# Three more seven-product groups and a shorter drain of the low banks in a hybrid decoder layer on one core

## The reference

```
hdn    = square(relu(x1 @ w_ff1))          # 256 x 8192, w_ff1 2048 x 8192
ff_out = hdn @ w_ff2                       # 256 x 2048, w_ff2 8192 x 2048
out    = layer_norm(ALPHA * x1 + ff_out)
```

## Time and profile before

| | |
|---|---|
| median of three runs | 1090.41 us (1090.23 to 1090.50) |
| the profiled execution, its time | 1090.53 us |
| the profiled execution, its span | 1088.5 us |
| PE busy | 1083.7 us of the span |
| DVE busy | 809.6 us, 74% |
| ACT busy | 571.7 us, 53% |
| mean HBM rate | 196 GB/s |

### The profile page before, as it was taken

How to read it: one execution, slowest core, us unless ns; L and a number is a source line. 1 busy time by engine, 2 the same in 40 slices (tenths; PEclk the granted TensorE clock), 3 DMA queues, 4 the chain that set the end, 5 groups by cost and what they waited for, 6 DMA issues and landing times.

```text
span 1088.5 us, 13897 instructions
## 1 busy us (share of the span) xinstructions
PE 1083.7 (100%) x5595; PEld 920.1 (85%) x5595; DVE 809.6 (74%) x890; ACT 571.7 (53%) x723; POOL 24.6 (2%) x43
## 2 busy tenths in 40 slices
PE   9999999999999999999999999999999999999998
PEld 8888888888888888888888888888888888888886
DVE  6587757666656685676699898666776678889998
ACT  6487757565554524445465454344454455554561
POOL 1000101010000000000000000000000000000000
PEclk9999999999999999999999999999999999999999
DMA  9857655557555825665756557466656655655762
GB/s 304 262 181 223 188 182 160 177 177 240 174 163 169 291 93 167 188 188 177 228 176 231 194 195 243 155 190 189 190 176 208 209 181 195 231 193 192 279 224 78
DMA packets 108047, 213.83 MB, mean 196 GB/s; under 512 B 6784, under 2 KB 38016, under 8 KB 107472
## 3 DMA queue, kind: packets, MB, share of 16 engines
q1 hardware_dynamic: 107216, 209.61, 59.5%
q0 software_dynamic: 624, 3.21, 1.0%
q10 hardware_dynamic: 144, 0.13, 0.0%
HBM read 210.83 MB, written 2.10 MB: 196 GB/s over the span
## 4 chain that ended last, share of the span: by engine, by line
PE 98%; DVE 1%; DMA 0%; issue 0%; ACT 0%; DVEq 0%
PE low_ps L797 11%; PE low_ps L634 10%; PE high_ps L797 9%; PE high_ps L817 8%; PE high_ps L818 8%; PE high_ps L819 8%; PE low_ps L526 6%; PE low_ps L522 6%; PE low_ps L524 6%; PE low_ps L803 5%; PE high_ps L803 5%; PE low_ps L639 5%; PE low_ps L817 2%; PE low_ps L818 2%; PE low_ps L819 2%; PE high_ps L571 1%
## 5 line engine op out<-in xcount | busy, mean ns | idle before, releaser
L1303 DVE TENSOR_TENSOR w_lo<-w_raw,w_hi 128x1024 fp32r<-128x1024 f32 x175 | 213.3, 1223 | 134.9 <-ACT w_hi L976 133.4
L976 ACT ACTIVATE w_hi<-w_raw 128x1024 fp32r<-128x1024 f32 x175 | 185.2, 1059 | 189.5 <-PE low_ps L526 68.9
L797 PE MATMUL low_ps<-x1T,w_hi 128*128 128x512 f32 x512 | 177.3, 393 | 0.0
L797 PE MATMUL high_ps<-x1T,w_hi 128*128 128x512 f32 x448 | 155.0, 393 | 0.0
L634 PE MATMUL low_ps<-xT,w_hi 128*128 128x512 f32 x448 | 144.2, 398 | 0.0
L803 PE MATMUL low_ps<-x1T,w_lo 128*128 128x256 f32 x512 | 139.3, 278 | 0.0
L1627 DVE TENSOR_TENSOR w_lo<-w_raw,w_hi 128x1024 fp32r<-128x1024 f32 x72 | 87.1, 1223 | 64.6 <-ACT w_hi L1175 64.6
L1175 ACT ACTIVATE w_hi<-w_raw 128x1024 fp32r<-128x1024 f32 x72 | 76.1, 1059 | 88.8 <-PE low_ps L797 43.4
L803 PE MATMUL high_ps<-x1T,w_lo 128*128 128x256 f32 x448 | 122.1, 278 | 0.0
L818 PE MATMUL high_ps<-w_lo,hid 128*128 128x512 f32 x290 | 112.4, 388 | 0.0
L819 PE MATMUL high_ps<-w_hi,hid 128*128 128x512 f32 x290 | 112.4, 388 | 0.0
(11 more groups left out here) (218 smaller groups left out, 1908.0 us busy)
## 6 DMA issues: line engine op xcount, KB each, us to landing
w_raw<-in_w_ff SPq DMA_DIRECT2D x208, 512.0 KB, 4.4
w_raw<-in_w_in SPq DMA_DIRECT2D x93, 512.0 KB, 4.1
more_raw<-in_w_ff SPq DMA_DIRECT2D x42, 512.0 KB, 5.3
w_raw<-in_w_out SPq DMA_DIRECT2D x32, 512.0 KB, 3.7
x_raw<-in_x_turned SPq DMA_DIRECT2D x8, 256.0 KB, 6.3
y<-in_x SPq DMA_DIRECT2D x8, 256.0 KB, 4.5
side_raw<-in_w_ff SPq DMA_DIRECT2D x4, 512.0 KB, 7.0
w_raw<-in_w_in SPq DMA_DIRECT2D x6, 256.0 KB, 5.2
```

Source lines behind the costliest of these rows:

```text
L797: return pe.matmul(banks[:, b, :], w_hi[:, slot, cols], x1T[:, t, :, :].rearrange("p h t -> p (h t)"), start=(t == 0 and not lows_open), s ...
L976: act.activation(w_hi[:, slot, :], w_raw[:, slot, :], ACT.Copy).then_inc(w_rounded, units)
L1303: dve.tensor_tensor(w_lo[:, slot, :], w_raw[:, slot, :], w_hi[:, slot, :].bitcast(F32), ALU.subtract).then_inc(w_split, units)
```

## The change

Thirty pairs are fast instead of 27: chunk 1 gives both of its pairs (`DOUBLE`), and the exception for the chunk `MIXED` falls, so passes 0 to 3 have 7, 7, 8 and 8 fast pairs. Since plain pairs fill the places between, a pass now ends in one plain pair where pass 0 ended in three: pass 0 runs F4 p0 F6 p2 F10 p8 F14 p12 F18 p16 F22 p20 F26 p24, and pass 1 opens with F4. Pass 2 ends F58 p62, where it ended F54 p58 p60 p62, and pass 3, which opens with F30, is as before.

The drain is in two steps. `copy_first` waits for the second mark of the last fast pair, after its fifth product, not the third. `drain_low` is three operations into a larger `mid` and frees the banks; `add_low`, one operation of 128 x 2048, adds `mid` to `y1` later (in passes 1 and 3 five or six pairs into the pass, for the one before). The scaling by `ALPHA` moves into `add_high`. In `end_pass` the splits of the last plain pair come ahead of the drain, and the splits of the next plain pair are put among the high additions. `small`, `ident_t`, `diag` and some buffers move in memory.

```diff
-MIXED = CHUNKS_FF - 2
-BLOCKS = [12 if c == MIXED else 11 if c in FAST_CHUNKS else 8 for c in range(CHUNKS_FF)]
+DOUBLE = 1
+FAST_PAIRS = [t for c in FAST_CHUNKS for t in ((TPC * c, TPC * c + 2) if c == DOUBLE else (TPC * c + 2,))]
+BLOCKS = [2 * TPC + 3 * len([t for t in FAST_PAIRS if t // TPC == c]) for c in range(CHUNKS_FF)]
...
         def copy_first(p):
 
-            act.wait_ge(fast_used, 3 * FAST_END[p])
+            act.wait_ge(fast_used, 3 * FAST_END[p] - 1)
             if p:
-                act.wait_ge(low_drained, p)
-            act.activation(mid[:, 0, :], low_ps[:, 0, :], ACT.Copy).then_inc(first_copied, 1)
+                act.wait_ge(low_added, p)
+            act.activation(mid[:, 1, :], low_ps[:, 0, :], ACT.Copy).then_inc(first_copied, 1)
+
+        def next_pass(p):
+
+            q = PASS_END[p]
+            round_pair(q - 1)
+            copy_first(p)
+            round_sums(q)
+            round_own(q)
...
         def drain_low(p):
 
+            dve.wait_ge(first_copied, p + 1)
+            dve.tensor_tensor(mid[:, 0, :], mid[:, 1, :], low_ps[:, 3, :], ALU.subtract).then_inc(
+                mid_made, 1)
+            dve.wait_ge(mid_made, 2 * p + 1)
+            dve.tensor_tensor(mid[:, 3, :], mid[:, 0, :], low_ps[:, 2, :], ALU.subtract).then_inc(
+                mid_made, 1)
+            dve.wait_ge(mid_made, 2 * p + 2)
+            dve.tensor_tensor(mid[:, 0:4:2, :], low_ps[:, 1:2, :].to_broadcast([P, 2, NC]),
+                              mid[:, 0:4:3, :], ALU.subtract).then_inc(low_drained, 1)
...
+        def add_low(p):
+
+            dve.wait_ge(low_drained, p + 1)
+            if p < len(PASSES) - 1:
+                dve.wait_ge(y2_summed, 3 * (p + 1))
+            mine = y1[:, :, half_of(p)]
+            dve.tensor_tensor(mine, mine, mid[:, :, :].rearrange("p (t b) n -> p t (b n)", t=TT),
+                              ALU.add).then_inc(low_added, 1)
...
+        HIGH = [(3, 1), (0, 2), (2, 1)]
 
         def end_pass(p):
 
             q = PASS_END[p]
+            split_pair(q - 1)
             drain_low(p)
             sum_pair(q)
-            split_pair(q - 1)
             split_sums(q)
             split_own(q)
-            add_high(p)
+            add_high(p, HIGH[:2])
+            split_plain(q + 1, (0,))
+            add_high(p, HIGH[2:])
+            split_plain(q + 1, (1,))
...
         for q in range(6, PART_END):
+            if q == PASS_START[1] + 6:
+                add_low(0)
             if q == PASS_END[0] - 1:
                 end_pass(0)
-            elif q == PASS_END[1] - 1:
-                drain_low(1)
+            elif q not in (PASS_START[1], PASS_START[1] + 1):
                 split_pair(q)
-            elif q != PASS_START[1]:
-                split_pair(q)
+        drain_low(1)
```

More of the change, by code:

```diff
@@ L80, in pass_order @@
     tiles = [t for c in range(*FF_PARTS[part]) for t in (TPC * c, TPC * c + 2)]
[L81 removed]
+    fast = [t for t in tiles if t in FAST_PAIRS]
     opens_plain = (part, half) == (1, 0)
[L83 to L84 removed]
     plain = [t for t in tiles if t not in fast]
@@ L173, in hybrid_layer @@
     relu = at("relu", [P, TT, NC], F32, 48 * KB)
[L174 to L181, removed]
+    hidden = at("hidden", [P, 14, P], F32, 48 * KB)
+    mid = at("mid", [P, 2 * TT, NC], F32, 48 * KB)
+    diag = [at(f"diag{tt}", [P, P], F32, 48 * KB + 512 * tt) for tt in range(TT)]
+    X0 = 56 * KB
     x1T = at("x1T", [P, KT, 2, SEQ], F32R, X0)
@@ L838, in fast_group @@
             part, half = PASSES[p]
-            c, g = t // TPC, NTH[q]
+            c, g, b = t // TPC, NTH[q], 2 * (t % TPC)
+            more = 8 if b else 11
             first, last = g == (FAST_END[p - 1] if p else 0), g == FAST_END[p] - 1
@@ L891, in plain_group @@
                 for tt in range(TT):
+                    if (n, tt) == (0, 0) and not begun:
+                        high_free(p, 0)
+                    if (n, tt) == (0, 1) and NTH[q] == (PLAIN_END[p - 1] if p else 0):
+                        high_free(p, 2)
                     for half in range(2):
@@ L1195, in round_sums @@
             g = NTH[q]
[L1196 to L1200, removed]
+            for n in range(2):
+                cols = slice(2 * n * NC, 2 * (n + 1) * NC)
+                act.wait_ge(fast_summed, 3 * g + (1, 3)[n])
+                act.activation(sum_hi[:, cols], sum_raw[:, cols], ACT.Copy).then_inc(fast_rounded, 1)
         def round_own(q):
@@ L1608, in square_hidden @@
             dve.wait_ge(hid_powered, f + 1)
[L1609 to L1616, removed]
+            pairs = [t for t in FAST_PAIRS if t // TPC == i]
+            for t in pairs:
+                n, b = FAST_PAIRS.index(t), 2 * (t % TPC)
+                more = 8 if b else 11
+                dve.tensor_tensor(hidden[:, more:more + 2, :],
+                                  hidden[:, b + 1:b + 2, :].to_broadcast([P, 2, P]),
+                                  hidden[:, b:b + 4:3, :], ALU.subtract).then_inc(hid_formed, 1)
+                dve.wait_ge(hid_formed, 2 * n + 1)
+                dve.tensor_tensor(hidden[:, more + 2, :], hidden[:, b, :], hidden[:, more + 1, :],
+                                  ALU.subtract).then_inc(hid_formed, 1)
+                dve.wait_ge(hid_formed, 2 * n + 2)
+                ins = dve.tensor_tensor(hidden[:, b + 1, :], hidden[:, b + 2, :], hidden[:, more + 2, :],
+                                        ALU.subtract)
+            ins.then_inc(hid_squared, 1)
         def split_hidden(i):
@@ L1636, in split_plain @@
                 dve.wait_ge(plain_used, PLAIN_END[2] + LAST_AFTER)
-            for b in range(2):
+            for b in which:
                 cols = slice(b * HALF, (b + 1) * HALF)
@@ L1686, in drain_low @@
         def drain_low(p):
-            part, half = PASSES[p]
[L1689 to L1696, removed]
@@ L1714, in add_high @@
             dve.wait_ge(plain_used, PLAIN_END[p])
-            for first, count in ((3, 1), (0, 2), (2, 1)):
-                col = PASSES[p][1] * HALF + (first % 2) * NC
+            for first, count in blocks:
+                col = half * HALF + (first % 2) * NC
                 mine = y1[:, first // 2, col:col + count * NC].rearrange("p (b n) -> p b n", b=count)
-                dve.tensor_tensor(mine, mine, high_ps[:, first:first + count, :], ALU.add).then_inc(
-                    y2_summed, 1)
+                dve.scalar_tensor_tensor(out=mine, in0=mine, scalar=1.0 if part else ALPHA,
+                                         in1=high_ps[:, first:first + count, :], op0=ALU.mult,
+                                         op1=ALU.add).then_inc(y2_summed, 1)
```

80 lines of the change are left out of this document (41 added, 39 removed).

## The result

The change took 1094.09 us (median of five runs, 1093.98 to 1094.90) against 1090.41 for the kernel before beside it: the ratio is 1.0034, 95% interval 1.0023 to 1.0046. Forecast was 1094.5, in 1092.3 to 1096.4.

A forecast was written before the change was run, and what follows sets the result against it. PE was taken to bound the kernel, busy 1083.7 of 1088.5 us. -2.04 + 2 x 2.89 + 0.1 + 0.2 = +4.04 us on 1090.53 gave 1094.6, less 0.12 for the median: 1094.5 us, range 1092.3 to 1096.4.

The forecast's parts named there:

- PE bound, and the gain 2.04 us: PE bounds the kernel throughout; three pairs made fast take nine matmuls off it in passes 0 to 3, saving 2.04 us.
- The chain at the ends of passes 0 and 2: Copy, drain, sums and splits there make PE 2.89 us late by the second fast pair of the next pass.
- The drain's dependent operations: Drain after passes 0 and 2: each operation waits for the one before; 512-element starts 0.73 us apart, not 0.60.
- The start of PE behind a split, 0.15 us: At the starts of passes 1 and 3, PE starts 0.15 us after the end of what it waits for.
- Catching up: Later in passes 1 and 3, DVE gains 1.06 us per two pairs; `add_low` still costs 0.1 and 0.2 us.
- The sum: Whole kernel: -2.04 + 2 x 2.89 + 0.1 + 0.2 = +4.04 us, giving 1094.5 us as median.
- What would show it: PE's list has some 6 us of waits, mostly early in passes 1 and 3; wrong if under 4 us.
- What costs nothing: Ends of passes 1 and 3, and `add_low` of pass 1: no waits; low banks free at 3.9, chunk starts 7.03.
- The rivals: Pass ends: waits small, 1088.4 us, 7%; part hidden, 1092, 9%; DVE not catching up, 1096, 12%; PE clock falls, 1104, 3%.
- The clock fell: Waits at pass ends put one fast pair at half pace, 4.8 us for each end: 1104 us; chance 3%.
- The third rival: Passes 1 and 3: DVE operations 1% longer, about 0.7 us of waits for each pass, 1096 us; chance 12%.

The follow-up runs named there:

- e4: The change with drain, high additions and late addition of passes 0 and 2 on 8 columns per block instead of 512: 1088.39 us, ratio 0.9979.
- e1: The change with the next fast pair's three sums ahead of the drain at the ends of passes 0 and 2: 1090.24 us, ratio 0.9995.
- e2: The change with only the first of the three sums ahead of the drain: 1091.84 us, ratio 1.0012.
- e3: The change with the copy of low bank 0 waiting for the last fast pair's third mark, 1.36 us later: 1097.02 us, ratio 1.0059.
- e5: The change with the late addition of passes 0 and 2 on 8 columns of each half: 1094.10 us, ratio 1.0035.
- e6: The change with the drain, high additions and copy mark of the kernel before, and `add_low` an empty step: 1102.93 us, ratio 1.0115.
- e7: The change with the 27 fast pairs of the kernel before, keeping the new drain and pass-end order: 1094.30 us, ratio 1.0035.
- e8: The change with ACT copying all four low banks and DVE combining the copies over the next pass: 1089.92 us, ratio 0.9996.
- e10: e1 with the late addition of passes 0 and 2 on GpSimd instead of DVE: 1100.72 us, ratio 1.0092.

## Why the prediction was right, point by point

- **PE bound, and the gain 2.04 us.** Right. e4, with the waits gone, is 2.19 us faster than before, and 2.04 by the starts in the passes.
- **The chain at the ends of passes 0 and 2.** Right, step by step, as the table shows. That it is the cause, and not the amount of DVE's work, is shown by e1 and e2 (order alone: -3.85 and -2.25 us), e3 (+2.9 for a later head) and e5 (4 us of DVE work elsewhere: nothing).
- **The drain's dependent operations.** Their starts are 0.72 apart, near the 0.73 of the rows, and not 0.60. The rule of the Trainium skill (VectorE: DVE Perf Modes, The DRAIN you can't avoid), that a semaphore costs nothing extra, would have made the drain 0.24 us too short at each end; here the measurement decides against it.
- **The start of PE behind a split, 0.15 us.** Right for the first split (621.41 against its end at 621.26), too long for `own`, where PE starts 0.05 after the split's end (624.44 against 624.39; 635.89 against 635.84). The forecast has no term for the matmuls behind a wait, of which the first comes 0.11 late each time. The two errors cancel, which is luck: 2.89 an end was forecast, 2.80 is measured at the product named, and 3.0 once the steps behind it are counted.
- **Catching up.** The late addition was put at 0.1 and 0.2 us of waits. Against e5, which takes nearly all of it out, it costs 0.04 and 0.18 by the starts, too little to show in the medians; the step of 0.11 over the pace at 1023, in pass 3, is gone in e5.
- **The sum.** +4.04 us was worked out; the starts give +4.1 in the passes and the medians +3.68. The 0.4 us by which 1094.5 was too high are therefore not a term of the sum, and are inside what these runs can tell.
- **What would show it.** Two of the signs did not come as written. PE's list has 2.6 + 0.8 = 3.4 us at the splits, not some 6, and by the letter that is under the 4 us that were to mean "I am wrong"; it has no entry for the high additions. The list takes a wait only from the modelled end of the matmul ahead, 0.39 us after its start, and leaves out the 0.16 us before that at each wait and the late matmuls behind. By the starts the waits are 6.1 us, and the high additions are the step of 0.47 at 626.17. The sign should have been written for the starts. The others came: the longest step is 1.11, nearly all lie within 25 us of the starts of passes 1 and 3, DVE idles 2.80 us ahead of L1714, no wait is for a load, and the granted clock is 1.00.
- **What costs nothing.** Right for the ends of passes 1 and 3. e6 shows how near the first was: with the longer drain PE waits 1.5 us there.
- **The rivals.** None came true. The clock fell in e6 behind a wait that the change does not have. The third rival was priced too high by its own figures: 71.1 us and 1% are 71.8, which is 0.4 over PE's 71.4 and not 0.7. A fact that I had not priced is that the new drain and order do as much harm with 27 pairs (e7): I held the three plain pairs of before to be the margin, and did not ask what the last plain pair's rounding ahead of the copy, and its split ahead of the drain, would do with them.

## What to carry to other kernels

When a serial piece of work shrinks, look at what is queued behind it on its engine and at what stands ahead: here DVE idled 2.8 us before a drain with three sums queued behind it, the first of them ready, and putting them first gave back 3.85 us. Price a removed instruction by the room that it leaves as well: nine matmuls saved 2.04 us, and the plain pairs that went from between two fast ones took 10.9 us of cover at each of two places. Such cover serves only if the work starts at its mark: in e7 it was there, and the drain started 9.6 us late. And once the bound engine is relieved, ask where the end of the kernel gets its time: e8 took every wait from PE and still gave back about two thirds of the gain to DVE's last chain.

## What the hardware showed that was not expected

- Between independent DVE operations of 1024 elements the starts are 1.13 to 1.14 us apart (616.32 to 617.46 in the change), and 1.25 where the second waits for the first (617.46 to 618.71 in the change); for 512 elements they are 0.60 and 0.72 (614.88 to 615.60).
- A wait of 4.04 us on PE was followed by twelve slow steps, all but the first of 0.427 us (granted clock 0.50), and then the full pace (e6); the waits of 0.4 to 0.7 us in the change and of 1.8 us in e3 were not.
- PE's first matmul behind a wait for the `own` split starts 0.05 us after that split's end, and the second 0.11 us later than at full pace (the change).
- GpSimd's addition of 2048 float32 elements with two SBUF inputs took 5.46 us, where DVE's takes 2.29, and held a DVE operation with two SBUF inputs that began after it for about its whole length (5.63 for 1.22 us, e10).
